# A two-layer encoder in float32: attention done by pairs of chunks, with the transposes placed between projection matmuls

## The reference, cut to what matters

```python
def swa_layer(x, w_in, w_out, sinks, k_band, v_band, bias, key_valid):
    q, gate = jnp.split(x @ w_in, 2, axis=-1)
    q = q.reshape(bsz, nc, CHUNK, SWA_KV_HEADS, SWA_GROUP, SWA_HEAD_DIM) * SWA_HEAD_DIM ** -0.5
    sc = jnp.einsum('bncvgd,bnkvd->bvgnck', q, k_band) + bias[None, :, :, None]
    sc = jnp.where(key_valid[:, None, :], sc, NEG_INF)
    m = jnp.maximum(sc.max(-1, keepdims=True), sink)
    p = jnp.exp(sc - m)
    p = p / (p.sum(-1, keepdims=True) + jnp.exp(sink - m))
    o = jnp.einsum('bvgnck,bnkvd->bncvgd', p, v_band).reshape(bsz, s, SWA_WIDTH)
    return (o * jax.nn.silu(gate)) @ w_out
```

## Time and profile before

| | |
|---|---|
| median of 3 runs | 2372.67 us (2370.01 to 2373.64) |
| span of the profiled execution, which is its own device time | 2370.2 us |
| PE busy in it | 98% of the span |
| DVE, ACT, POOL busy | 75%, 50%, 14% |

### The profile page before, as it was taken

The page is one execution under the profiler, slowest core; times in us unless marked ns, Lnnn a source line. Parts: engine busy times, 40 slices in busy tenths (PEclk is TensorE's granted clock), DMA queues, the critical chain, the costliest instruction groups (busy, mean ns, idle before and its releaser), DMA issues.

```text
span 2370.2 us, 31112 instructions
## 1 busy us (share of the span) xinstructions
PE 2316.1 (98%) x11554; PEld 1893.0 (80%) x11554; DVE 1779.2 (75%) x2575; ACT 1178.2 (50%) x1757; POOL 329.1 (14%) x346
## 2 busy tenths in 40 slices
PE   8999999999999999999999999999999999999996
PEld 6878878877788888887788888888777888888775
DVE  7878798866857669876796776896588668788458
ACT  4344455357435445536654554553665445553463
POOL 2212211122010111112201001110210110011032
PEclk9999999999999999999999999999999999999998
DMA  8787668653725445864483444575257335454423
GB/s 304 265 281 243 233 223 293 223 181 127 255 90 177 147 131 172 296 207 167 144 278 130 160 161 143 177 266 178 72 186 254 128 126 162 132 204 148 119 72 124
DMA packets 211798, 437.10 MB, mean 184 GB/s; under 512 B 14848, under 2 KB 52240, under 8 KB 208064
## 3 DMA queue, kind: packets, MB, share of 16 engines
q1 hardware_dynamic: 197568, 369.28, 47.0%
q0 software_dynamic: 14080, 65.83, 7.6%
HBM read 373.45 MB, written 57.41 MB: 182 GB/s over the span
## 4 chain that ended last, share of the span: by engine, by line
PE 78%; DVE 10%; DMA 5%; issue 4%; ACT 2%; SPq 0%; POOL 0%; DVEq 0%; ACTq 0%; POOLq 0%
PE accs L693 22%; PE accs L694 21%; PE accs L695 21%; DVE w_lo L1396 3%; PE bank L693 3%; PE bank L695 3%; PE bank L694 3%; DMA stage<-ret_w_in 2%; PE bank L959 2%; PE bank L968 1%; DMA stage<-t_prep 1%; PE bank L978 1%; PE bank L799 1%; DVE z L1721 1%; ACT w_hi L1044 1%
## 5 line engine op out<-in xcount | busy, mean ns | idle before, releaser
L1396 DVE TENSOR_TENSOR w_lo<-stage,w_hi 128x1024 fp32r<-128x1024 f32 x524 | 649.8, 1247 | 350.5 <-ACT w_hi L1044 349.2
L1044 ACT ACTIVATE w_hi<-stage 128x1024 fp32r<-128x1024 f32 x524 | 550.5, 1056 | 488.8 <-PE accs L695 174.1
L693 PE MATMUL accs<-w_hi,xs 128*128 128x512 f32 x1136 | 450.0, 396 | 10.1 <-ACT sg L1049 4.1
L695 PE MATMUL accs<-w_hi,xs 128*128 128x512 f32 x1136 | 443.1, 390 | 0.0
L694 PE MATMUL accs<-w_lo,xs 128*128 128x512 f32 x1136 | 442.5, 390 | 0.0
L693 PEld LDWEIGHTS accs<-w_hi,xs 128*128 128x128 f32 x1136 | 213.5, 188 | 59.5 <-issue 11.6
L695 PEld LDWEIGHTS accs<-w_hi,xs 128*128 128x128 f32 x1136 | 213.2, 188 | 45.4
L694 PEld LDWEIGHTS accs<-w_lo,xs 128*128 128x128 f32 x1136 | 213.7, 188 | 42.2
L693 PE MATMUL accs<-x_hi,w_hi 128*128 128x512 f32 (+1 forms) x640 | 245.4, 384 | 1.2 <-ACT sgT L1049 0.7
L694 PE MATMUL accs<-x_lo,w_hi 128*128 128x512 f32 (+1 forms) x640 | 237.5, 371 | 0.0
L695 PE MATMUL accs<-x_hi,w_lo 128*128 128x512 f32 (+1 forms) x640 | 235.9, 369 | 0.0
(11 more groups left out here) (205 smaller groups left out, 3807.9 us busy)
## 6 DMA issues: line engine op xcount, KB each, us to landing
stage<-t_prep SPq DMA_DIRECT2D x208, 512.0 KB, 4.4
stage<-ret_w_in SPq DMA_DIRECT2D x100, 512.0 KB, 3.9
stage<-ret_w_in SPq DMA_DIRECT2D x128, 256.0 KB, 2.9
stage<-swa_w_in SPq DMA_DIRECT2D x64, 512.0 KB, 4.2
t_prep<-t_buf POOLq DMA_DIRECT2D x28, 1024.0 KB, 5.6
stage<-ret_w_out SPq DMA_DIRECT2D x48, 512.0 KB, 3.7
cs<-rope_t SPq DMA_DIRECT2D x16, 1024.0 KB, 7.4
t_buf<-ret_w_in POOLq DMA_DIRECT2D x32, 512.0 KB, 8.4
```

Of the source, the lines that this page charges most:

```text
L693: mm(dst, lhs[0], rhs[0], start=start, stop=False, skip_group_check=reopened)
L695: return mm(dst, lhs[1], rhs[0], start=False, stop=stop, skip_group_check=reopened)
L1044: copy(w_hi[:, RING[g] % HS], stage[:, RING[g] % LS], ACT.Copy).then_inc(w_hi_made, 1)
L1396: nc.vector.tensor_tensor(w_lo[:, RING[g] % LS], stage[:, RING[g] % LS], w_hi[:, RING[g] % HS].bitcast(F32), sub).then_inc(w_split, 1)
```

## The change

The 16 units of a block become 8 pairs of neighbouring chunks. One visit belongs to one slot: visits 0 to 10 to the slots Q1 to G1+2.

- Behind a slot's first half PE issues the transposes of one unit, the scores of a whole pair and the value products of a whole pair; behind its second half the transposes of the pair's other unit, alone.
- The softmax works on a pair at a time: tiles `pr`, `lowest`, `rsum`, `rinv` are twice as wide, the bias and sink operands are broadcast over the two units; POOL multiplies a pair in two instructions, and ACT does the exponentials in two groups of four with the second copy of transposes between them.
- The queries of Q1 are emptied by DVE alone (four instructions instead of two and two), and the gate of G0 is copied out by DVE; ACT applies SiLU to that copy one slot later, in two instructions, and signals `g0_gated`, for which POOL waits.
- `prT` has four buffers in the room of `qrT`/`krT`, which `sum_hi` shares, so the first copy into it waits for the stores of the sums; `bias` moves into the room of `kk_hi`/`kk_lo`.
- `make_hi` of a visit's slot stands at the slot's start, `make_lo` behind the softmax and the emptying.

```diff
-STEPS = NU + 3
-def step_place(k):
-    if k < 4:
-        return Q1 + k, 1
-    if k < NU:
-        return G0 + (k - 4) // 2, (k - 4) % 2
-    return [(G1 + 2, 0), (G1 + 2, 1), (G1 + 3, 0)][k - NU]
+NPR = NU // 2
+VISITS = NPR + 3
+def visit(p):
+    return p - Q1 if 0 <= p - Q1 < VISITS else None
...
+            def turn_probabilities(s, u):
+                pe.wait_ge(p_normed, NU * s + u + 1)
+                need(pe, pT_copied, NU * s + u)
...
+            def score_pair(s, j):
+                if j == 0:
+                    pe.wait_ge(kv_moved, 80 * (s + 1))
...
+                for b in range(2):
+                    g, c = UNITS[2 * j + b]
...
+            def attend(s, j, second):
+                u = 2 * (j - 2) + second
+                if 0 <= u < NU:
+                    turn_probabilities(s, u)
+                if not second and j < NPR:
+                    score_pair(s, j)
+                if not second and j >= 3:
+                    weigh_pair(s, j - 3)
...
-                            for k in range(STEPS):
-                                if step_place(k) == (p, u):
-                                    attend(s, k)
+                            if visit(p) is not None:
+                                attend(s, visit(p), u)
...
+                    if visit(p) is not None:
+                        k = visit(p)
+                        if 2 <= k < NPR + 2:
+                            copy_turned(s, 2 * (k - 2))
+                        if k >= 3:
+                            copy_weighed(s, k - 3)
+                        if k < NPR:
+                            exponentials(s, k, 0)
+                        if p == G1:
...
+                                copy(gate_part, gate_part, ACT.Silu).then_inc(g0_gated, 1)
+                        if 2 <= k < NPR + 2:
+                            copy_turned(s, 2 * (k - 2) + 1)
+                        if k < NPR:
+                            exponentials(s, k, 1)
...
+                    if visit(p) is not None and visit(p) <= NPR:
+                        if visit(p) > 0:
+                            softmax_back(s, visit(p) - 1)
+                        if visit(p) < NPR:
+                            softmax_front(s, visit(p))
+                        if p == Q1 + 3:
+                            for m in range(4):
+                                query_out(s, p, 1, m)
+                        if p == G0 + 3:
...
+                                nc.vector.tensor_copy(sgT[:, :, m, :], acc[m].rearrange("p (c q) -> p c q", q=CHUNK))\
+                                    .then_inc(acc_free[m], 1)
+                        make_lo(ahead(g))
```

More of the change, by code:

```diff
@@ L957, in attend, with weigh_pair @@
                         rows = slice(e * HD, (e + 1) * HD)
-                        mm = nc.tensor.matmul(bank[4 + 3 * e][:, (i // 2) * BAND:(i // 2 + 1) * BAND],
+                        at_ = (2 * b + i // 2) * BAND
+                        mm = nc.tensor.matmul(bank[4 + 3 * e][:, at_:at_ + BAND],
                                               qT[rows, c, 2 * kvh:2 * kvh + 2, :].rearrange("p a q -> p (a q)"),
                                               kT[rows, kvh, c * CHUNK:c * CHUNK + BAND], start=True, stop=True)
[L962 to L971, removed]
+                mm.then_inc(s_full, 1)
+            def weigh_pair(s, j):
+                pe.wait_ge(pT_copied, NU * s + 2 * j + 2)
+                need(pe, o_copied, NPR * s + j)
+                for b in range(2):
+                    u = 2 * j + b
                     g, c = UNITS[u]
-                    pe.wait_ge(pT_copied, NU * s + u + 1)
-                    need(pe, o_copied, NU * s + u)
                     val = vt[:, (c - 1) // 2, :] if c % 2 else vs[:, c // 2, :]
@@ L1170, in turn_x1_hi, with copy_turned, copy_weighed, exponentials @@
                          bank[4 + u % 4][:].rearrange("p (e n) -> p e n", e=4), ACT.Copy).then_inc(x1_hi_made, 1)
+            def copy_turned(s, u):
+                act.wait_ge(pT_full, NU * s + u + 1)
+                if u == 0 and s + 1 < NS:
+                    wait_sums_stored(act, s + 1)
+                need(act, o_full, NPR * s + u // 2 - 1)
+                copy(prT[:, u % 4, :], bank[5][:], ACT.Copy).then_inc(pT_copied, 1)
+            def copy_weighed(s, j):
+                g, c = UNITS[2 * j]
+                act.wait_ge(o_full, NPR * s + j + 1)
+                copy(qT[:, c:c + 2, 4 * g:4 * g + 4, :],
+                     bank[6][:].rearrange("p (c a q) -> p c a q", c=2, a=4), ACT.Copy).then_inc(o_copied, 1)
+            def exponentials(s, j, b):
+                if b == 0:
+                    act.wait_ge(lowest_ready, NPR * s + j + 1)
+                    need(act, p_inv, NPR * s + j)
+                for i in range(4):
+                    scores, n = pr[:, j % 3, b, i, 0:BAND + 1], 4 * b + i
+                    exped = copy(scores, scores, ACT.Exp, bias=lowest[:, n:n + 1], scale=-1.0,
+                                 accum_out=rsum[:, n:n + 1])
+                if b == 1:
+                    exped.then_inc(p_exped, 1)
             for w in range(4):
@@ L1329, in _ @@
[L1329 removed]
+                            empty(s, Q0, m, qT[:, :, m, :], scale=-HD ** -0.5, last=p).then_inc(acc_free[m], 1)
                         make_hi(ahead(g))
[L1331 to L1360 removed]
@@ new lines, in softmax_back, with query_out @@
+            def softmax_back(s, j):
+                need(dve, p_inv, NPR * s + j)
+                dve.wait_ge(p_exped, NPR * s + j + 1)
+                if j >= 2:
+                    dve.wait_ge(p_normed, NU * s + 2 * j - 2)
+                nc.vector.reciprocal(rinv[:, j % 2, :], rsum[:]).then_inc(p_inv, 1)
+            def query_out(s, p, c, m):
+                dve.wait_ge(products, full(s, p, m))
+                nc.vector.tensor_scalar(qT[:, :, 4 * c + m, :], acc[m].rearrange("p (c q) -> p c q", q=CHUNK),
+                                        -HD ** -0.5, None, ALU.mult).then_inc(acc_free[m], 1)
```

177 lines of the change are left out of this document (65 added, 112 removed).

## The result

The changed kernel takes 2347.8 us (median of 4 runs, 2345.9 to 2351.8), beside 2371.9 for the kernel before: a ratio of 0.9901, 95% interval 0.9888 to 0.9914. It is faster by 24 us.

The account below looks back on a forecast made before the run. PE, busy 98% of the span, was taken as the bound. 24.6 - 4.4 - 2.8 - 1.8 = 15.6 us off the profiled 2370.2 gives 2354.6; with 2.5 for the median, 2357 us, range 2349 to 2366.

Parts of the forecast that it names:

- The units: PE time each kind of visit adds between projection matmuls, from start spacings: 0.44 to 2.79 us.
- A full visit: Visits 3 to 7, with transposes, sixteen scores and sixteen values behind a first half: 2.79 us each.
- the rival of 4 us more: Going from scores to values needs no change of shape, so regrouping saves 4 us more: 2353 us, chance 0.08.
- The gain: Regrouping saves 5.98 us per block, 23.9 in four, plus 0.7 for the SiLU wait at G1: 24.6 us.
- the flat 0.23: Spacing in us taken between starts of projection matmuls, the same before and after the change.
- old step: One full attention group between projections in the kernel before: 2.02 us beyond undisturbed projections, 13 per block.
- The first scores: They come half a slot earlier and wait for the key/value DMA: 1.7 us block 0, 2.7 more block 1; 4.4 lost.
- The clock: Block 1's 4.3 us idling is followed by a stretch at 1.2 GHz: 2.8 us lost once, bounds 0 and 3.4.
- the rival "the clock holds": No fall to 1.2 GHz follows block 1's wait at the first scores: 2354 us, chance 0.17.
- DVE at the change of banks: Emptying behind the softmax at Q1+3 comes 0.9 us late in blocks 0 and 1: 1.8 us lost, bounds 0 and 10.4.
- the prediction's clock: Time counted from the start of a visit's last score matmul; first emptying done at 3.7 us, PE wanting it at 4.56.
- A cost at nothing: POOL's multiplications, exponentials and second transposes' copy end in time; that copy frees bank 5 at 5.2 us, wanted at 7.3.

Follow-up runs that it names:

- kv_late: Changed kernel with the five DMAs that place keys and values issued one slot later, in Q0+3 instead of Q0+2: 2367.1 us, one execution.
- after_third: The changed kernel timed and profiled a third time, nothing edited: 2349.6 us, ratio 0.9903 to the kernel before.
- sink_first: Changed kernel with DVE's sink copy moved ahead of the two additions, directly behind the reciprocal that starts POOL's multiplications: 2347.3 us, ratio 0.9899 to the kernel before.
- after_again: The changed kernel timed and profiled a second time, nothing edited: 2348.7 us, ratio 0.9896 to the kernel before.
- act_banks: Changed kernel with ACT again emptying two of four query banks and applying SiLU straight from G0's gate banks: 2366.5 us, ratio 0.9985 to the kernel before.

## Why the prediction was right and wrong

The mechanism held: time was won by what stands next to what, and the waits appeared where they were forecast. Two terms of the sum were wrong in size: the wait at block 1's first scores, with the fall of the clock that hung on it, and the gain.

- **The units held.** A full visit 2.75 (2.79), a visit of scores 1.29 (1.30), with transposes 1.73 (1.74), values and transposes 1.66 (1.69), values alone 1.22 (1.25), transposes alone 0.44 (0.44). Scores to values cost a change of shape, 0.2, as taken; the rival of 4 us more came close in size, but not by its cause.
- **The gain was mis-sized, 24.6 for 27.8.** Block 2 won 6.96, not 5.98 and the 0.2 of its SiLU wait. The step is the flat 0.23 for every projection beside the groups: behind each group the next ones start 0.229 to 0.233 apart, 0.227 undisturbed, and more so behind the old steps. Summed over the projections of the block, this excess is 1.0 us before and 0.5 after. Reckoned with 0.227, an old step costs 2.026 and not 2.02, and a full visit 2.76 and not 2.79; that makes most of the rest.
- **The first scores: 4.4 forecast, 2.2 found.** By the starts the waits are 1.76 and 2.03, less 1.6 that block 1 had before. Block 0's, 1.69 by PE's idle time, is as forecast (1.7), in part by luck: the same kernel idled 2.37 and 1.77 there in its two other profiles. Block 1's is 1.95, not 4.3. This step failed: it took the landing seen in one execution as fixed against Q1, and it moves by microseconds; 1.66 to 3.26 was found. What sets that issue can be followed in the traces, though no edit tried it. SP's queue stands at a store of sums until DVE has made their low part, DVE has a weight's low part to make first and waits for ACT's high part, and ACT waits until that weight has landed. From that store to the issue of `vs<-vcar` pass 8.7 to 9.1 us in the kernel before and in all eight executions. ACT's copy and SP's issue in block 1, before, then after:

```profile
1050.36 1.06 ACT L1044 ACTIVATE w_hi<-stage 128x1024 fp32r<-128x1024 f32 x1 [5.51 <-DMA stage<-swa_w_in]
1062.91 0.82 SPq L678 DMA_DIRECT2D vs<-vcar  x1
...
1041.53 1.06 ACT L1052 ACTIVATE w_hi<-stage 128x1024 fp32r<-128x1024 f32 x1 [2.48 <-DMA stage<-swa_w_in]
1053.83 0.92 SPq L671 DMA_DIRECT2D vs<-vcar  x1
```

The copy begins 10.1 us ahead of Q1 before and 12.5 ahead of it after: one weight landed 2.3 us earlier against Q1. Why it did stays open.

- **The clock: 2.8 forecast, 0 in the profiled execution.** It hung on the same 4.3. The mechanism is there: kv_late paid 3.0 in block 2, and after_third fell in blocks 0 and 1. The rival "the clock holds" was thus right for that profile alone. The condition was too strict, though: block 0's 1.7, costed at nothing, was followed by a fall in after_third (1.77) and sink_first (1.82).
- **DVE at the change of banks: 1.8 forecast, 1.76 found**, at the places named, 1.06 in block 0 and 0.70 in block 1. The cause was also as forecast: the sink copy beside POOL, as sink_first shows. In block 0, DVE's additions begin 0.43 later than in block 2, the copy takes 1.37 longer, and the first bank is empty at 5.37 on the prediction's clock, not at 3.60; PE wants it at 4.45. That the sum comes so close is partly luck: 0.9 was a choice between 0 and 1.3. And the 2.27 of the earlier trace rows was misread as more than one multiplication: that copy ran beside one longer POOL instruction, the product with the gate (L2172, 2.39 us from 557.97 on), and ended with it. The Trainium skill, page "SBUF — State Buffer", section "Who interferes with whom", says that the later of the two is blocked for the whole instruction of the other; the prediction worked out from it a loss of at most one multiplication of 1.04. The copy took 1.54, until both had ended. The measurement decides.
- **A cost at nothing that wasn't:** the copy of the second transposes, with 2.1 to spare, was late by 0.70 and 0.14 at visit 3 in blocks 0 and 1. The condition had been named (DVE late by more), its price left out.

In sum, for the stretches, by the starts: 27.8 - 2.2 - 0 - 1.8 - 0.8 = 23.0, as measured. Of the 7.4 us that the forecast missed there, 5.0 are block 1's wait and the clock on it, 3.2 the gain, less 0.8 for the copy. The 2.5 outside the stretches had no term in the forecast; they are less than the 7.9 by which that part differs between profiles of the changed kernel.

## What to carry to other kernels

Where an engine is busy for the whole span, time is still won by what stands next to what: price a regrouping from start to start, and include the ten instructions behind each group. A wait taken from one execution for a transfer is a sample; look in the trace for what sets the moment of issue before multiplying it into a sum. And before a wait is removed, ask what else is late underneath: here two edits that removed it made the kernel slower, and one that moved the whole chain by half a slot did not.

## What was unexpected of the hardware

- Projections of one shape start 0.229 to 0.233 us apart on average for some ten matmuls behind an attention group, 0.227 otherwise. The cause stays open.
- Idling of PE of about the same length was followed by 1.2 GHz in one execution and not in another: 1.69 us (no) and 1.77 (yes) at block 0's first scores, 1.95 (no) and 2.05 (yes) at block 1's. At these two places the longest without a fall was 2.37 (after_again), the shortest with one 1.66 (act_banks).
- A DVE copy of 128x8 that takes 0.17 us alone took up to 1.93 us beside POOL; in all 14 profiles of the changed kernel and its edits, every copy of over 0.25 us ended within 0.05 us of the second of POOL's two multiplications.
